# Loading the retention tables earlier and the weights later at each change of head, and a second weight block ahead of x tiles 4 to 7 at the start of a hybrid decoder step

## The reference

```python
h = rms_norm(x, norm_g)
z = h @ w_in                      # 13312 columns
# A: retention, 4 heads of 256: q, k rotary; chunks of 128 tokens
s = einsum('bihd,bjhd->bhij', qc, kc) * inner
o = einsum(s, vc) + einsum(qc, S) * q_dec ; S = S * chunk_dec + k_dec*k^T v
y_ret = (rmsnorm(o) * silu(rg)) @ w_ret_o
# B: conv: pre = cc * cu ; y = (cb * conv3(pre) * silu(cg)) @ w_conv_o
# M: 4-head cross attention into 256 memory tokens, then @ w_mem_o
merged = g_ret * y_ret + g_conv * y_conv + g_mem * y_mem     # gates from h
y = x + merged @ w_out ; final rms_norm
```

## Time and profile before

| | us |
|---|---|
| median of 3 runs | 1230.22 |
| all runs | 1230.22, 1379.27, 1229.18 |
| profiled execution, whole time | 1226.59 |
| its span on cores 0 to 7 | 1218.3, 1223.3, 1224.1, 1207.2, 1215.6, 1223.8, 1224.8, 1221.0 |
| PE busy on core 6, share of its span | 1161.5, 95% |
| ACT, DVE and POOL busy on core 6 | 477.0, 587.0, 336.2 |

### The profile page before, as it was taken

One profiled execution on the slowest core, in us unless ns is written; L12 is line 12 of the kernel. 1 busy time (PEld: TensorE's weight loads), 2 busy tenths in 40 slices (PEclk: granted clock), 3 DMA queues, 4 the chain that ended last, 5 costly groups with the idle time before them and its releaser, 6 DMA issues.

```text
span 1224.8 us, 22082 instructions; the slowest of 8 cores (1207.2 to 1224.8 us)
## 1 busy us (share of the span) xinstructions
PE 1161.5 (95%) x7114; PEld 594.5 (49%) x7239; DVE 587.0 (48%) x1026; ACT 477.0 (39%) x1007; POOL 336.2 (27%) x399
## 2 busy tenths in 40 slices
PE   6799999999999999999999999899799799999997
PEld 3545444455554555555444544455355345444443
DVE  3674455442222366556222367566576476312276
ACT  3442233222222444444222256465365366322243
POOL 3432222221000111010333435435334344333300
PEclk9899999999999999999999999999899899999999
DMA  9554111112555786874322043824724634811074
GB/s 225 162 119 73 35 35 36 35 36 39 104 103 104 141 141 103 150 125 83 104 54 43 3 121 130 213 87 162 181 102 150 178 121 120 251 35 35 1 243 186
DMA packets 38430, 133.79 MB, mean 109 GB/s; under 512 B 4784, under 2 KB 9008, under 8 KB 33584
## 3 DMA queue, kind: packets, MB, share of 16 engines
q0 software_dynamic: 10512, 56.63, 27.6%
q1 hardware_dynamic: 27808, 75.77, 18.6%
HBM read 160.03 MB, written 28.98 MB: 154 GB/s over the span
## 4 chain that ended last, share of the span: by engine, by line
PE 78%; DMA 7%; DVE 5%; issue 4%; ACT 2%; POOL 2%; SPq 1%; DVEq 0%; ACTq 0%; POOLq 0%
PE psf L424 71%; DMA pms<-c_qdecX 5%; PE psh L424 5%; PE psh L427 2%; DMA mgd<-xp 2%; DMA arF<-c_cos 1%; ACT th L1022 1%; DVE tf L1194 1%; DVE gaux L1295 1%; DVE arF L1396 1%; DVE th L1031 1%; POOL th L1349 1%; DVE ssb L1018 0%; DVE xbuf L1295 0%; POOL th L1197 0%
## 5 line engine op out<-in xcount | busy, mean ns | idle before, releaser
L424 PE MATMUL psf<-hT,w 128*128 128x512 bf16 (+1 forms) x3304 | 632.5, 342 | 10.0 <-DVE tf L1194 2.3
L424 PEld LDWEIGHTS psf<-hT,w 128*128 128x128 bf16 x3392 | 298.3, 98 | 303.9 <-issue 13.2
L424 PE MATMUL psf<-ob,w 128*128 128x512 bf16 (+1 forms) x901 | 183.8, 346 | 0.2
L600 ACT ACTIVATE tf<-psf,hbg 128x512 f32<-128x512 f32 (+1 forms) x89 | 56.3, 633 | 188.7 <-PE psf L424 184.0
L424 PEld LDWEIGHTS psf<-ob,w 128*128 128x128 bf16 x904 | 81.7, 98 | 84.9
L615 POOL TENSOR_TENSOR mgd<-tf,mgd 128x512 bf16<-128x512 f32 (+1 forms) x79 | 78.8, 1007 | 156.0 <-DVE tf L611 156.0
L611 DVE SCALAR_TENSOR_TENSOR tf<-tf,psf 128x512 f32<-128x512 f32 (+1 forms) x72 | 43.5, 604 | 155.5 <-PE psf L424 145.2
L424 PE MATMUL psf<-w,hT 128*128 128x512 bf16 (+1 forms) x483 | 112.1, 383 | 1.0 <-ACT th L1022 0.8
L1197 POOL TENSOR_TENSOR th<-tf 128x512 bf16<-128x512 f32 x32 | 40.7, 1272 | 141.3 <-DVE tf L1194 141.3
L424 PEld LDWEIGHTS psf<-w,hT 128*128 128x128 bf16 x488 | 48.0, 100 | 54.4 <-issue 6.2
L400 POOL DMA_DIRECT2D w<-wb x37 | 21.1, 570 | 176.0 <-PE psf L424 175.2
(11 more groups left out here) (218 smaller groups left out, 1316.2 us busy)
## 6 DMA issues: line engine op xcount, KB each, us to landing
w<-wb POOLq DMA_DIRECT2D x37, 1024.0 KB, 8.9
mgd<-xp SPq DMA_DIRECT2D x16, 512.0 KB, 8.9
arH<-cmk POOLq DMA_DIRECT2D x12, 512.0 KB, 14.6
arH<-cmv POOLq DMA_DIRECT2D x10, 512.0 KB, 10.2
gaux<-sret SPq DMA_DIRECT2D x8, 512.0 KB, 4.9
xbuf<-sret SPq DMA_DIRECT2D x8, 512.0 KB, 7.2
stgt<-sret SPq DMA_DIRECT2D x8, 512.0 KB, 4.0
hbt<-sret SPq DMA_DIRECT2D x8, 512.0 KB, 5.3
```

Source lines behind the costliest of these rows:

```text
L424: P.op('pe', lambda e: e.matmul(out, lhsT=lhsT, rhs=rhs, start=start, stop=stop), reads=reads, writes=[wbuf])
L600: P.op('act', lambda e, fg=fg, ti=ti, n=n, bcol=bcol: e.activation(out=tf[ti][:, 0:n], in_=psf[fg][:, 0:n], func=AF.Tanh, bias=hbg[:, bcol ...
```

## The change

It does four things.

1. **Change of head, tables.** `tables` is split. `table_q(h + 1)` issues qdecX and now maskSf as well, and it stands right behind the k projection of turn g = 3; `table_m(h + 1)` issues maskX at the old place.
2. **Change of head, weights.** At g = 3 of heads 0 to 2 the two blocks are only counted as used. They are issued one each behind the k projection in the turns g = 1 and g = 2 of the next head. Head 3 issues two blocks of the projection behind it in that way.
3. **Start, order.** Block 1 is issued, in two halves, right behind the four parts of block 0. Tiles 4 to 8 are loaded when tile 3 has been squared (before: 4 to 7 when tile 2 has). A second bank (fc0, the cc group) is filled tile by tile beside fu0. Items run (0,0), (1,0), (0,1), (1,1): item (1,0) on block 1 takes the place in which tiles 4 to 7 are prepared, and item (0,1) uses 32 matmuls of 512 columns in place of 128 of 128 columns. Four of the 35 warming matmuls go.
4. **Packing.** The quarters of the convolution blocks are packed as cu, cc, cb, cg, so that the parts arrive in the order of use.

```diff
-        blocks.append([("w_in", 4096 + q * 1024 + c * 128, 128, q * 128) for q in range(4)])
+        blocks.append([("w_in", 4096 + q * 1024 + c * 128, 128, i * 128) for i, q in enumerate((0, 2, 1, 3))])
...
-            if t == 1:
-                for _ in range(4):
-                    x_load(after=[B_xs[2]])
-            elif t > 1:
+            if t == 2:
+                for _ in range(5):
+                    x_load(after=[B_xs[3]])
+            elif t > 2:
                 x_load()
...
         x_mul()
         x_sq()
+        wpart(1, 0, 2)
+        wpart(1, 2, 4)
         fu0 = falloc()
+        fc0 = falloc()
         x_tr()
         warm(3)
-        x_sq()
         x_mul()
...
-        warm(2)
+        tile_mm(fc0, 1, 0)
         x_tr()
         tile_mm(fu0, 0, 2)
+        tile_mm(fc0, 1, 1)
+        tile_mm(fc0, 1, 2)
         tile_mm(fu0, 0, 3)
+        tile_mm(fc0, 1, 3)
...
-        def slot_a(si, post):
...
+        def slot_b(si, post):
+            if post:
                 x_mul()
+                if si < 3:
+                    x_sq()
+            elif si == 3:
                 x_tr()
-
-        conv_item(0, 0, W0, BW0, 0, 0, slot=slot_a, banks={0: fu0})
-        P.tag = 'conv'
-        fb = {q: falloc() for q in (0, 2, 1, 3)}
-        x_sq()
-        x_tr()
-        for t in range(4, 8):
-            if t < 6:
-                x_mul()
-                x_tr()
-            for q in (0, 2, 1, 3):
-                tile_mm(fb[q], q, t)
...
-        conv_item(0, 1, W0, BW0, 0, 0, slot=x_slot, banks=fb)
-        for (c, g, lim) in ((1, 0, 10), (1, 1, 12), (0, 2, 14), ...
+        conv_item(0, 0, W0, BW0, 0, 0, banks={0: fu0, 1: fc0})
+        x_sq()
+        conv_item(1, 0, W1, BW1, 1, 1, slot=slot_b)
+        x_tr()
+        x_tr()
+        x_tr()
+        x_sq()
+        x_mul()
+        x_sq()
+        for (c, g, lim) in ((0, 1, 10), (1, 1, 12), (0, 2, 14), ...
...
-        def tables(h):
+        def table_q(h):
             more = [B_qx] if h == 0 else []
             P.op('sp', ... qdecX ...)
+            P.op('sp', ... maskSf ...)
+
+        def table_m(h):
+            more = [B_qx] if h == 0 else []
             P.op('sp', ... maskX ...)
...
             ki = prot(i, 256, mid_k)
+            if g == 3 and h < 3:
+                table_q(h + 1)
+            if h > 0 and 1 <= g <= 2:
+                wissue(wstate['done'] + NSLOT - 2 + g)
...
-            if g == 3:
+            if g == 3 and h < 3:
+                wstate['done'] += 2
+            elif g == 3:
                 wdone()
                 wdone()
             r_scores(ki, qi)
...
             if g == 3 and h < 3:
-                tables(h + 1)
+                table_m(h + 1)
```

More of the change, by code:

```diff
@@ L402, in wissue, with wpart @@
                 wstate['issued'] += 1
[L404 to L407, removed]
+        def wpart(i, q0, q1, after=()):
+            P.op('pool', lambda e: e.dma_start(out=wsl[i][:].rearrange("p k n -> p (k n)")[:, q0 * 1024:q1 * 1024],
+                                               in_=wb[i][:, q0 * 1024:q1 * 1024]),
+                 reads=list(after), writes=B_w[i][q0:q1], dma_sem='w%dq%d' % (i, q0))
         def wget():
@@ L545, in warm @@
                 mm(psf[fwarm][:], qms[:, 0:128], qms[:, 128:640], True, True, [B_mx], B_psf[fwarm])
-        warm(28)
-        wquarter(0, after=[B_xr[0]])
+        warm(26)
+        wpart(0, 0, 1, after=[B_xr[0]])
         x_sq()
-        wquarter(2)
+        wpart(0, 1, 2)
         x_sq()
-        wquarter(1)
+        wpart(0, 2, 3)
         x_mul()
         x_sq()
-        wquarter(3)
+        wpart(0, 3, 4)
         x_mul()
         x_sq()
+        wpart(1, 0, 2)
+        wpart(1, 2, 4)
         fu0 = falloc()
+        fc0 = falloc()
         x_tr()
         warm(3)
-        x_sq()
         x_mul()
@@ L695, in conv_item @@
                 fcu = grp(0, 0)
-                fcc = grp(1, 2)
+                fcc = grp(1, 1)
                 t_cu = tfa()
@@ L728, in conv_item @@
                     reads=Bp + RC, writes=[B_tf[t_cv]])
-                fcb = grp(2, 1)
+                fcb = grp(2, 2)
                 P.op('dve', lambda e, t_cv=t_cv, m1=m1, n=n, c=c, v3=v3: e.scalar_tensor_tensor(
@@ L753, in conv_item @@
                                                               in_=preS[:, :, 8:10]), reads=Bp, writes=BL_nct)
-        wstate['issued'] = 1
+        wstate['issued'] = 2
         wstate['next'] = 2
@@ L758, in build_nc @@
         W1, BW1 = W4[1], B_w[1]
-        def slot_a(si, post):
-            if post and si == 0:
+        def slot_b(si, post):
+            if post:
                 x_mul()
-            elif post and si == 1:
-                x_sq()
-            elif post and si == 2:
-                x_mul()
-                x_sq()
-                wissue(2)
-            elif not post and si == 3:
-                x_tr()
-        conv_item(0, 0, W0, BW0, 0, 0, slot=slot_a, banks={0: fu0})
-        P.tag = 'conv'
-        fb = {q: falloc() for q in (0, 2, 1, 3)}
-        x_sq()
-        x_tr()
-        for t in range(4, 8):
-            if t < 6:
-                x_mul()
-                x_tr()
-            for q in (0, 2, 1, 3):
-                tile_mm(fb[q], q, t)
+                if si < 3:
+                    x_sq()
+            elif si == 3:
+                x_tr()
         def x_slot(si, post):
@@ L794, in x_slot @@
                     x_sq()
-        x0['lim'] = 0
-        conv_item(0, 1, W0, BW0, 0, 0, slot=x_slot, banks=fb)
-        for (c, g, lim) in ((1, 0, 10), (1, 1, 12), (0, 2, 14), (1, 2, 16), (0, 3, 17), (1, 3, 17), (0, 4, 17), (1, 4, 17)):
+        conv_item(0, 0, W0, BW0, 0, 0, banks={0: fu0, 1: fc0})
[7 more added lines that the diff above has]
+        x_sq()
+        for (c, g, lim) in ((0, 1, 10), (1, 1, 12), (0, 2, 14), (1, 2, 16), (0, 3, 17), (1, 3, 17), (0, 4, 17), (1, 4, 17)):
             x0['lim'] = lim
@@ L1169, in ret_w @@
             return wret[h]
-        def tables(h):
+        def table_q(h):
             more = [B_qx] if h == 0 else []
             P.op('sp', lambda e: e.dma_start(out=qdecX, in_=c_qdecX[h].partition_broadcast(128)), writes=[B_qd] + more, dma_sem='hcq')
+            P.op('sp', lambda e: e.dma_start(out=maskSf, in_=c_maskSf[h]), writes=BL_maskSf, dma_sem='hc3')
+        def table_m(h):
+            more = [B_qx] if h == 0 else []
             P.op('sp', lambda e: e.dma_start(out=maskX, in_=c_maskX[h]), writes=[B_mk] + more, dma_sem='hcm')
@@ L1213, in samp_a @@
             WA, BWA, WB, BWB = ret_w(h)
-            P.op('sp', lambda e: e.dma_start(out=maskSf, in_=c_maskSf[h]), writes=BL_maskSf, dma_sem='hc3')
             fq = falloc()
@@ L1436, in build_nc @@
         load_cs(0)
-        tables(0)
+        table_q(0)
+        table_m(0)
         P.tag = 'ret'
```

## The result

| | before | after |
|---|---|---|
| median of the runs, us | 1229.93 (4 runs) | 1215.61 (4 runs) |
| profiled execution, us | 1226.59 | 1214.75 |
| spans of cores 0 to 7 | see above | 1205.9, 1201.2, 1211.0, 1202.9, 1210.5, 1202.7, 1212.9, 1205.7 |

The ratio is 0.9886, with an interval from 0.9866 to 0.9905. That is a real gain of 1.1%, and less than the 2% that count as faster. It lies within the forecast range, 9.6 us above the forecast's own figure. A gain of the forecast size was there, and two costs were larger than forecast.

A forecast was written before the change was run, and what follows sets the result against it. PE was taken to bound the kernel (95% of the span), with gains only where it waits or clocks low. 1224.8 - 24.7 (heads) + 3 (sines) - 0.5 (start) = 1202.6 span, 1204.4 profiled, 1206 us with half the median's extra; range 1197 to 1217.

The forecast's parts named there:

- The gain at the heads: At changes of head, removing table and sines stalls behind weight blocks brings the slowest core from 1224.8 to 1200.1: 24.7 us.
- The tables at nothing: At the change of head, issuing qdecX earlier in the program gains nothing, since SP is in order: 0 us.
- The landing of 4 to 8 us: At the change of head, qdecX lands within 4 to 8 us once no weights pass with it, against 18.7.
- the sample turn of 23.6 us: The loop turn with the samples' work, 31.0 us, takes 23.6 without 5.6 of waiting and 1.8 of low clock.
- The sines behind a block: In turns g = 1 and 2, sines issued behind a moved block stall DVE about 3 us; bounds 0 and 18.
- The start: Up to item (0,2), gains and losses of the new order nearly cancel: -0.5 us, starting at 63.5 instead of 64.03.
- PE's idle time, today 13.1 us, is again ... 10.5 us: At the start: 0.5 (block 1) + 0.7 (its second half) + 4.6 (psh) + 4.7 (tile 8), then about 3 us low clock.
- The extra of the median over the profile: The runs' median lay 3.6 us above the profiled execution; half of that was added, giving 1206 us.
- The sines and state loads take the stall over: Rival: moved blocks delay sines in 3 of 6 turns at 3 us, plus state loads: 12 us, time 1215; chance 0.18.
- No new stall: Rival: cosines land in time everywhere in g = 1 and 2, start gains some us: 1200 or 1197; chance 0.26.
- Nothing at the heads: Rival: the table is late by its own queue, so only the start counts: about 1230 us; chance 0.06.
- slower: Rival: sines stall in all six turns on the slowest core, 45 us lost at 7.5 each: 1248 us; chance 0.03.

The follow-up runs named there:

- e3: Kernel before plus the head changes alone (old start), each moved weight block also waiting on POOL for the next turn's sines: 1202.38 us, ratio 0.9768.
- e5: Kernel before with only the tables moved behind the k projection; both weight blocks still go out at the change of head: 1229.32 us, ratio 0.9992.
- e4: Kernel before with only the weight blocks moved to turns g = 1 and 2, all tables at their old place: 1212.23 us, ratio 0.9843.
- s5: e3 with weight block 1 issued in two halves right behind block 0, old order of items: 1205.96 us, ratio 0.9787 to the kernel before.
- s2: Whole change with moved blocks waiting for the sines, plus tile 8 prepared between transposes of tiles 5 to 7: 1205.16 us, ratio 0.9803 to the kernel before.
- s3: Whole change with moved blocks waiting for the sines, but tiles 4 to 7 loaded as in the kernel before: 1207.47 us, ratio 0.9819 to that kernel.
- s4: The edits of s2 and s3 together, moved blocks waiting for the sines: 1205.43 us, ratio 0.9780 to the kernel before.
- e1: Kernel before with the two changes at the heads alone (tables split, weights in g = 1 and 2), old start: 1210.57 us, ratio 0.9834.

## Why the prediction was right, and where it was not

**The gain at the heads: right, in place and size.** 26.5 us too many were counted on core 6 and 20.9 on core 7. Core 6 gave back 26.1, and in e3 every core takes 257.8 where the prediction had 258. The span forecast for a kernel with no stall at the heads and the old start, 1200.1 us, is what e3 shows (1201.1). That the stalls are in both forms, table and sines, and go together, is shown by e3; on core 6 of e5 they even took the form of the sines in place of the table.

**The tables at nothing: right.** e4 and e5 show it from both sides. The landing of 4 to 8 us came out at 5.2 to 7.8 us over all cores and changes, the sample turn of 23.6 us at 23.3. The reason given holds too: in e5 on core 6 qdecX goes out 0.05 us behind the weight block, as before.

**The sines behind a block: the mechanism was right, the size was not.** The term was 3 us, one stall on the slowest core. The one stall came, on cores 2, 4 and 6, and cost 7.7 us. That it was one in six places was an estimate of the prediction ("the lower third") that came true; which cores have it is decided by some 0.1 us in the order of two issues. Two things were left out. First, the landing: 9.5 us were taken, measured 12.2. The block's own work was right: the queues of core 6 from 994 to 1004 us (packets, MB, share of 16 engines) show it taking 62.3% of 10 us, 6.2 us, against 6.3 in the prediction. But first comes a gap: the DMA row of that window (busy tenths in slices of 0.25 us) stands at 0 for the first 1.75 us, and 117 packets in 0.24 MB make 2 KB each, so that the 256 KB of sines are 128 packets and 11 were still to pass at 1004.

```profile
DMA  0000000279349955999669285989994998599997
...
q0 software_dynamic: 126, 1.02, 62.3%
q1 hardware_dynamic: 117, 0.24, 14.3%
```

Second, the clock. PE stood for 5.3 us and then worked at 1.2 GHz, which cost 1.8 us in the first 8 matmuls alone (3.57 against the 1.8 us that 8 take at 2.4 GHz), so 7.1 of the 7.7 us are accounted for by the two. The prediction had charged just that to the old stall and not to the new one. With its own 1.8 us and the right landing the term would have been 12.2 - 6.5 + 1.8 = 7.5.

By the Trainium skill, "DMA: Bandwidth & Descriptors", section "Queues, rings and completion order", an engine goes round its queues packet by packet, and drains a packet, typically 9 to 17 descriptors, before it switches. The trace agrees that the queues take turns once both are moving, 126 packets of weights against 117 of the other queue, each of the former with 0.79 us of an engine (62.3% of 10 us x 16 / 126). The unit differs: the profile counts 144 packets for one block, 9 for each engine, and these alternate one for one, 13 to 18 against 13 to 17 in each us from 997 to 1003. If the profile's packet is the page's descriptor, the turns here are shorter than the page has them. Nor is a transfer slowed wherever it shares the engines with weights: in g = 1 and 2 the sines that went out first were not (2.5 to 5.1 us). Turn-taking alone does not explain the step of "Last turn", nor the gap: on core 7 the sines move in the 2 us between the block's issue and its first packet, and on core 6, issued 0.40 us behind, they wait until the block moves. What holds them is open.

**The start: wrong.** Forecast -0.5 us, and a start of item (0,2) at 61 to 66 us on core 6. It came at 70.36, 6.3 us late, and 4.4 us late in the mean of the cores; the prediction named a move of over 4 us as what would prove it wrong. The places were right: idle ahead of tile 8, two waits for `psh`, clock 0.50 behind. The step that failed is "PE's idle time, today 13.1 us, is again ... 10.5 us", and three things are wrong with it:

- The 13.1 us hold 3.3 us of waiting for tiles 0, 1 and 3 and the 10.5 do not; those waits stay (after: 3.85 + 0.41 = 4.3 us). Like against like it was 10.5 + 3.3 = 13.8, already no gain. The three rows of the kernel before, core 6, that should have been counted:

```profile
11.76 0.61 PE L427 MATMUL psh<-idb,mgd 128*128 128x128 bf16 x8 [1.32 <-DVE mgd L493]
...
13.66 0.61 PE L427 MATMUL psh<-idb,mgd 128*128 128x128 bf16 x8 [0.64 <-DVE mgd L493]
...
18.85 0.61 PE L427 MATMUL psh<-idb,mgd 128*128 128x128 bf16 x8 [1.30 <-DVE mgd L493]
```

- Block 1 was put at 0.5 us and its second half at 0.7. On core 6 PE waits 2.7 us for it.
- Tiles 6 to 8 cost 3.28 + 2.25 + 5.02 = 10.55 us, put at 9.3.

That makes 4.3 + 2.7 + 10.55 = 17.5 us, as the list of waits after has it (9.3 + 5.5 + 2.7), against 13.1 before. The 13.1 leave out some short waits of before, 0.64 us for block 0 among them. All idle time counted, by the two rows of the stretch up to item (0,2), PE stands for 67.36 - 49.42 = 17.9 us against 61.00 - 46.49 = 14.5: 3.4 us more. The other 2.9 of the 6.3 us are PE's busy time, 49.42 against 46.49 us, at a mean granted clock of 0.82 against 0.94. One sees it in the rows: after, 15 matmuls take 5.91 us where 15 took 3.62 in the earlier trace rows, and 24 take 6.93 us where 24 x 3.62 / 16 = 5.4 would do. In the mean of the eight cores the start is 4.4 us later, and there the idle time alone grows by 4.5 us (13.0 to 17.5); PE's busy time stays (47.6 and 47.5), perhaps since the lower clock and the cheaper form of item (0,1) make up for each other; no run separates them. The step "as the parts nearly cancel" had no row behind it; the bound of the same paragraph, "6 us of DMA work and 3 us of low clock lost", was the nearer one.

What of it is which part: block 1 ahead of the tiles costs 2.3 us of start by s5, tile 8's chain gives 2.3 by s2, the loads 0.9 in the mean by s3. The sum, 5.5, is more than the 3.9 that the new start costs against e3, and s4 shows that the last two do not add. So two single causes are shown, and their shares beyond that stay open.

**The sum, with what the runs show.** 1224.8 - 26.1 (heads of core 6) + 7.7 (sines) + 6.4 (start) = 1212.8, measured 1212.9. The forecast's terms for the same were -24.7 + 3 - 0.5. The two costs are 11.6 us above their terms; that the forecast is out by 9.6 and not more owes something to luck, 1.4 us more from the heads of core 6 and 0.9 us less of the extra named below. The prediction had set the gain by core 7, because core 7 was to be the slowest without stalls; as it came, core 6 had both the latest start and the late sines. The extra of the median over the profile was 3.3 us before (1229.93 - 1226.59) and is 0.9 now (1215.61 - 1214.75); half of it was forecast to stay.

**Rivals.** "The sines and state loads take the stall over", 1215 us, is the nearest in time to 1215.6, but the working differs: it had three places at 3 us, and on core 6 it was one place at 7.7 and the start at 6.4. Its signs did show: DVE waited for sines on three cores, and turns above 19.5 us came on cores 0, 3 and 7 (19.7 to 20.3). e1 shows that the rival was no small matter: without the new start, the heads of six of eight cores take more than 259 us, up to 266.4. "No new stall", 1200 or 1197, is what e3 comes near to at 1202.4, by one wait more and with the old start. "Nothing at the heads" and "slower" fell.

## What to carry to other kernels

A bulk load and the small loads that are needed sooner share the DMA engines, so place the bulk load behind the landing of the small ones: a wait of the issuing queue on them cost nothing here and was worth 0.7% (e1 to e3), while moving the small load up in the program, on a queue where other loads still stood in front of it, was worth nothing. Do not rely on the order of two issues that lie a few tenths of a us apart: it differed from core to core, and it decided between 3 and 12 us. Whoever moves a stall must charge the new place what the old one was charged, the low clock behind it too. When an idle time "today" is compared with one counted from the new order, both have to hold the same waits.

## What the runs showed of the hardware

- A table of 64 KB takes 18.7 us with two weight blocks of 1 MB in flight and 6.4 us with none; 256 KB of sines take 12.2 us beside one block issued 0.4 us sooner, and 3.3 us on core 7 beside one issued 0.13 us sooner. In the packed stretches the two queues pass about one packet each in turn, and one of weights (8 KB) holds an engine for 0.72 to 0.79 us, one of the sines (2 KB) for 0.20 (14.3% of 10 us x 16 / 117).
- On core 6 nothing moves on the DMA engines in the first 1.75 us of the window that begins 0.3 us after the block's issue on POOL, though the sines were issued in it.
- A stall of PE of about 5 us costs about 7: at each of the places read here (5.59, 5.33 and 5.02 us) the matmuls behind it ran at 1.2 GHz. At 2.43 us, right behind two further waits, the same happened (s2). Behind the 2.99 us at 27.45 it did not: eight transposes took 0.61 us there.
